# Decayed keys and queries of the RWKV chunks made inside the first attention, in other storage

## The reference, cut to what matters

```
decay = exp(-exp(w_log));  a = sigmoid(aaa_bias + xa @ w_aaa_up)
kk = k * k_k, each head divided by its length
k = k * (1.0 + (a - 1.0) * k_a)
per token:  sa = state @ (-kk)
            state = state * decay + sa * (kk * a) + v * k
            y = state @ r
```

## Time and profile before

| | us |
|---|---|
| median of 3 runs (lowest to highest) | 1201.37 (1200.52 to 1203.36) |
| the profiled execution, its own time | 1199.54 |
| its span, first to last instruction | 1197.7 |
| PE busy | 1124.4 |
| DVE busy | 797.2 |
| ACT busy | 589.7 |
| POOL busy | 122.8 |

### The profile page before, as it was taken

The page is one execution under the profiler, slowest core; times in us unless marked ns, Lnnn a source line. Parts: engine busy times, 40 slices in busy tenths (PEclk is TensorE's granted clock), DMA queues, the critical chain, the costliest instruction groups (busy, mean ns, idle before and its releaser), DMA issues.

```text
span 1197.7 us, 18403 instructions
## 1 busy us (share of the span) xinstructions
PE 1124.4 (94%) x7620; PEld 918.8 (77%) x7620; DVE 797.2 (67%) x1319; ACT 589.7 (49%) x911; POOL 122.8 (10%) x122
## 2 busy tenths in 40 slices
PE   7898799999999999999998999999998799999997
PEld 5666678787888888887877778878777677888785
DVE  5647774658666776557567895778768868455644
ACT  6465333254556564465755644453563266345441
POOL 0404161400000000000000000003405400000000
PEclk9999799999999999999999999999998899999998
DMA  8522112224555455455322644555531244555551
GB/s 304 190 93 101 36 54 72 72 88 155 171 187 187 165 185 181 166 182 185 127 86 102 246 165 155 189 191 183 182 116 38 72 159 154 189 184 186 193 186 52
DMA packets 49668, 177.50 MB, mean 148 GB/s; under 512 B 5648, under 2 KB 6288, under 8 KB 49328
## 3 DMA queue, kind: packets, MB, share of 16 engines
q1 hardware_dynamic: 49584, 176.32, 42.1%
HBM read 175.25 MB, written 1.05 MB: 147 GB/s over the span
## 4 chain that ended last, share of the span: by engine, by line
PE 75%; DVE 13%; ACT 7%; issue 2%; POOL 1%; DMA 1%; SPq 0%; DVEq 0%; ACTq 0%
PE wps L2632 21%; PE wps L2634 20%; PE wps L2633 20%; PE tps L2621 4%; DVE wlo L1777 3%; ACT whi L1392 2%; DVE bt L2386 1%; PE tps L2862 1%; PE tps L2867 1%; DVE bt L2397 1%; POOL arena L2451 1%; PE tps L2678 1%; PE tps L3042 1%; DMA x<-in_x 1%; PE tps L2839 1%
## 5 line engine op out<-in xcount | busy, mean ns | idle before, releaser
L1777 DVE TENSOR_TENSOR wlo<-raw,whi 128x1024 fp32r<-128x1024 f32 (+1 forms) x322 | 390.5, 1237 | 170.3 <-ACT whi L1392 169.1
L2632 PE MATMUL wps<-whi,a_hi 128*128 128x512 f32 (+1 forms) x1008 | 404.4, 401 | 20.4 <-DVE a_lo L1799 8.4
L2634 PE MATMUL wps<-wlo,a_hi 128*128 128x512 f32 (+1 forms) x1008 | 395.1, 392 | 0.0
L2633 PE MATMUL wps<-whi,a_lo 128*128 128x512 f32 (+1 forms) x1008 | 394.4, 391 | 0.0
L1392 ACT ACTIVATE whi<-raw 128x1024 fp32r<-128x1024 f32 (+1 forms) x322 | 325.4, 1050 | 53.6 <-PE wps L2634 50.6
L2632 PEld LDWEIGHTS wps<-whi,a_hi 128*128 128x128 f32 x1008 | 191.5, 190 | 66.3 <-DVE wlo L1777 13.9
L2634 PEld LDWEIGHTS wps<-wlo,a_hi 128*128 128x128 f32 x1008 | 190.9, 189 | 40.5
L2633 PEld LDWEIGHTS wps<-whi,a_lo 128*128 128x128 f32 x1008 | 191.7, 190 | 36.7
L2632 PE MATMUL wps<-whi,f_hi 128*128 128x512 f32 x264 | 104.8, 397 | 0.0
L2634 PE MATMUL wps<-wlo,f_hi 128*128 128x512 f32 x264 | 104.3, 395 | 0.0
L2633 PE MATMUL wps<-whi,f_lo 128*128 128x512 f32 x264 | 104.3, 395 | 0.0
(11 more groups left out here) (404 smaller groups left out, 1261.9 us busy)
## 6 DMA issues: line engine op xcount, KB each, us to landing
raw<-in_w_dn SPq DMA_DIRECT2D x22, 512.0 KB, 3.2
raw<-in_w_0dn SPq DMA_DIRECT2D x22, 512.0 KB, 3.2
raw<-in_w_1dn SPq DMA_DIRECT2D x22, 512.0 KB, 3.2
raw<-in_w_ua SPq DMA_DIRECT2D x20, 512.0 KB, 3.2
raw<-in_w_ub SPq DMA_DIRECT2D x20, 512.0 KB, 3.6
raw<-in_w_0ug SPq DMA_DIRECT2D x20, 512.0 KB, 3.2
raw<-in_w_0uu SPq DMA_DIRECT2D x20, 512.0 KB, 3.3
raw<-in_w_1ug SPq DMA_DIRECT2D x20, 512.0 KB, 3.2
```

The costliest lines, as they stand in the source:

```text
L1777: V.tensor_tensor(t.wlo[n % NR][:, 0:w], t.raw[n % NR][:, 0:w], t.whi[n % NH][:, 0:w].bitcast(F32), ALU.subtract).then_inc(m.done(s.dve_lo ...
L2632: T.matmul(o, xh, wh, start=first, stop=False)
L2633: T.matmul(o, xl, wh, start=False, stop=False)
L2634: mm = T.matmul(o, xh, wl, start=False, stop=last)
```

## The change

`decayed` becomes a generator among the RWKV preparations, put behind the shifted tiles of `wr`, with two tiles at each of its two steps. It no longer waits for `heads_out` 1. `AR` moves to `h`, the tile of the residual stage, `btl` and `ktl` stay at 28 and 32 KB of the arena, where the attention had rotary scratch, and the probabilities that lay there get other storage. The `fill` behind the four `decayed` goes away with them.

```diff
+    def decayed_prep():
+        for t in range(4):
+            emit("decayed", t, z_parts["wr"])
+            if t % 2:
+                yield
+
...
-                                       ("wr", "zr", 512, 0, None), ("wv", "zv", 512, 8, bonus_prep)):
+                                       ("wr", "zr", 512, 0, decayed_prep), ("wv", "zv", 512, 8, bonus_prep)):
...
-    for t in range(4):
-        emit("decayed", t, z_parts["wr"])
-    fill(1)
...
-        t.mprob = [view(24, 384), view(25.5, 384), view(34, 384), sb("mprob3", [P, 384], F32, s1)[:, :]]
-        t.mprobT = [view(27, 384), view(28.5, 384)]
+        t.mprob = [view(24, 384), view(25.5, 384)] + [sb(f"mprob{i}", [P, 384], F32, s1)[:, :] for i in (2, 3)]
+        t.mprobT = [view(42, 384), sb("mprobT1", [P, 384], F32, s1)[:, :]]
...
-        t.AR = view(20, 2048).rearrange("p (t c a s) -> p t c a s", t=4, c=2, a=2)
+        t.AR = t.h[:, :, :].rearrange("p j c -> p (j c)").rearrange("p (t c a s) -> p t c a s", t=4, c=2, a=2)
...
     def decayed(i, z):
         dve.wait_ge(*m.at("ka"))
         dve.wait_ge(*m.at("Wn"))
-        dve.wait_ge(*m.at("heads_out", "m", 1))
...
     def decayed(i, z):
         pool.wait_ge(*m.at("k2"))
         pool.wait_ge(*m.at("Wn"))
-        pool.wait_ge(*m.at("heads_out", "m", 1))
```

## The result

The changed kernel takes 1205.43 us (median of 11 runs, 1203.39 to 1206.67) against 1201.09 for the kernel before (11 runs, 1198.11 to 1204.33). The medians differ by 4.3 us. The ratio is 1.0031, interval 1.0022 to 1.0040; 0.31% of the time is 3.7 us. The median lies outside the range given. The profiled execution has a span of 1202.0 us.

A forecast was written before the change was run, and what follows sets the result against it. PE was taken to bound the kernel, with DVE setting the pace at the attention's end. Terms -2.7 - 1.4 + 2.8 + 0.8 = -0.5 us gave 1200.9 us; forecast's own range 1199.2 to 1203.2, with outer cases 1198.0 to 1204.2.

The forecast's parts named there:

- DVE's queue: End of the first attention: DVE's twelve operations take 4.0 us there, making wv's tiles late by 3.9 us.
- The moved slab: Behind rwkv_out of chunk 1: a third slab with nothing to hide under, cost 2.8 us, bounds 0 and 3.0.
- So this wait hides behind DVE: In the attention: values 4 waits for heads_out 0's bank until 130.7 us, at no cost because DVE is later.
- parts two and three: DVE's operations lengthen the attention by 4.0 us; behind it key_tokens start 2.7 us earlier and the clock gains 1.4.
- An equal rise puts it near 140: End of the attention: PE's clock rises near 140 us, so key_tokens and pair scores gain 1.4 us.
- part four: Later slabs shift: one more uncovered behind rwkv_out of chunk 1 costs 2.8 us, the moved empty steps 0.8 together.
- +0.75 with the way there and back: Behind right_side of chunk 1, now without a slab: solve waits for ACT's copy of RU, cost 0.75 us.
- The signs: Wrong if key_tokens start outside 142 to 146, clock is low at g0's first slab, or y_mean outside 257 to 262.
- (2): Clock stays low through key_tokens, pair scores and following slabs: +3.7 us (1205.1), with two slabs +6.5; chance 0.10.
- (3): Attention ends as late as key_tokens start now: +2.2 us, up to +5.9 (1203.6 to 1207.3); chance 0.08.
- (1): Slab finds a hole, or DVE's twelve are hidden: -3.3 or -3.5 us (1198.1 or 1197.9); chance 0.18.
- the term of 0: POOL's early ktl beside DVE's split: split and copy grow 1.6 us, taken as free before DVE's 2.15 us idle.

The follow-up runs named there:

- e9: Changed kernel with all four decayed in the formerly empty step behind probs_T 4, no shifted steps, and the slab behind the attention kept; 1200.39 us, 0.9994 to before.
- e5: As e1, plus the two new preparation steps, which emit nothing; 1201.19 us, 0.9998 to before.
- e1: Changed kernel's new storage and no wait for heads_out, but decayed at its old place with its fill; 1199.0 us, 0.9975 to before.
- e12: Changed kernel plus 32 matmuls with unused results in PE's waits of the attention; 1203.93 us, 1.0013 to before.
- e3: Changed kernel with one slab more behind the takes at right_side of chunk 1, taken from the three at the end; 1201.06 us, 0.9996 to before.
- e4: The changed kernel run again, code unchanged; 1205.5 us, 1.0028 to before.
- e6: Against before: new storage, btl, ktl and AR's key half two steps after key_mix, query half behind heads_out 1; 1200.84 us, 0.9987.
- e10: Third profile of the kernel before, code unchanged; y_mean 143.3 us after the scores of heads 6 and 7, against 140.2 in the first profile.
- e13: e8 plus 7, 6 and 6 matmuls with unused results in PE's waits of the attention; 1196.30 us, 0.9958 to before.
- e8: e1 with DVE making btl ahead of AR, and each tile's pair scores waiting only for that tile's AR; 1196.47 us, 0.9963 to before.

## Why the prediction was wrong

**What held.** DVE's queue: the twelve operations stand 0.335 us apart between 130.02 and 135.01, with heads_out 0 in their middle; wv's tiles are 3.75 us late against the scores (forecast 3.9). key_tokens have no wait. Pair scores and key_tokens run at full clock, which gains 1.6 us (forecast 1.4). The moved slab turns up uncovered at the end, three in a row before y_mean. The wait ahead of solve is 0.90 us (forecast 0.75).

**"So this wait hides behind DVE" held too.** values 4 waited 2.65 us for the bank, but v_tokens began 16.07 us behind the scores, exactly as in e9, which has the operations and not the shift. What the prediction left out is that the shift costs something by itself: in e5, without the operations, v_tokens come 1.0 us later and the last values 2.3 later than in e1. How much of that is the bank (0.63 us of waiting), how much the order, and how much the clock, no run separates.

**First failed step, in parts two and three: "An equal rise puts it near 140".** The lower clock lasted from 128.2 to 145.3 us, 17.1 us where before has 10.3. Counted from the scores the rise came at 22.6 us; the forecast's 140 is 19.8. values 5 stood ahead of bonus_sum at half clock, and bonus_sum took 3.73 us where the sum had 2.2. The attention ended 5.0 us late in place of 4.0. I had carried the time of a rise over from one order of work to another. e12 shows that the low clock is the cause: with PE kept busy bonus_sum takes 1.97 and v_tokens 1.06, and the attention ends 2.4 us behind before. Why the rise comes so late stays open. It isn't the idle time alone: between the scores and v_tokens PE's waits add up to 8.5 us in e9 and to 7.8 in the change, and in e9 the clock rises at 19.0. Nor is it fixed by the code: in e3, with the same attention, it rose at 20.4, and the last values came 3.9 us late, which is the forecast.

**Second and larger, part four: "+0.75 with the way there and back".** The wait was priced, what it does to the clock was not. Solve ran at the lower clock, in part or wholly, and so did the slab behind it, in each of the three profiles of after and in e12; e3 puts a slab there and has neither. From right_side of chunk 1 to y_mean both kernels do the same work, four slabs among it: 19.9 us before (240.46 to 260.33), 22.3 after (242.35 to 264.69), so 2.5 us are lost there.

**The sum.** By the landmarks of the first profiles the pair scores are over 3.4 us earlier (forecast 4.1), the slab costs 2.8 as forecast, and the rest 2.5 (forecast 0.8): +1.9 for -0.5. The medians say +4.3 and the ratio +3.7. The first profile of before is one of the shortest. The four profiles of before have y_mean at 260.3, 259.9, 264.7 and 263.1 us from the start of the span (262.0 on average), the three of after at 264.7, 265.0 and 264.3 (264.7). That is 2.6, of which 1.5 lie ahead of the scores, where PE has the same work in both, and 1.1 behind them. What remains, 1.1 to 1.7 us, lies behind y_mean, where the code is the same. The 99 runs of before in the four later comparisons have 50 us of low clock each on average, the 23 of after in the first two 60 (2 x span x (1 - mean clock)); the first profile of before has 43 by this count and its second 41. Among the 99 runs of before themselves, those with 10 us more of low clock take about 2.5 us longer (a fitted line). So the rest goes together with low clock in other places; with so few profiles its cause stays open.

**The signs.** The prediction called itself wrong for key_tokens outside 142 to 146 us and y_mean outside 257 to 262 (its first transposes). As they stand, 147.3 and 263.8, both fall outside. With the 2.5 us by which the scores are late taken off, key_tokens (144.9) lie inside and y_mean (261.3) just inside. The clock is full at the first slab of g0.

**Rivals.** (2) named the clock but put it behind key_tokens, where it was full; low clock lasted longer ahead of them and came again 100 us later. That its price, 3.7 us, is the measured one is luck. (3), that key_tokens don't come earlier, is refuted: they came 1.8 us earlier. (1) is refuted: the operations were not hidden (e9, v_tokens 3.75 us late), and the slab cost its 2.8.

**The overlap with POOL.** The split is DVE L1780, beside POOL's four. In the first profile of after it began just ahead of POOL's third (120.05 and 120.10) and took 1.22 us; that POOL operation took 1.76 where the median is 0.74. In e4, the same code, it began behind POOL's third (120.41 and 120.25) and took 1.66, and in e1 1.71. In e6 two of DVE's operations took 0.94 to 0.96 in place of 0.41. That the later one waits is what the Trainium skill says ("SBUF — State Buffer", "Who interferes with whom"), and the trace agrees. DVE idled 1.70 us behind the split even in e4, and nobody waited for POOL, so the term of 0 held.

**The clock.** The Trainium skill's "TensorE: Matmul & The Clock Gate", Part 1, was weighed for a gain only. That idling drops the clock bears on the hole ahead of solve as well, and there it speaks against the change. The traces agree as far as they go: low clock followed the 0.90 us of waiting in four of four profiles. But e10 has it at right_side with no such wait, so the wait is not its only cause.

## What to carry to other kernels

Price a new wait of PE together with the clock behind it: here a hole of 0.9 us behind a chain of small matmuls cost about 2.5, and a slab put into it took that back. A step moved into a stretch where DVE sets the pace comes out at its full length; move what frees a buffer or an engine (here the wait and the storage) apart from the order, and measure the two alone, since here the first gained 0.25% and the second lost more than 0.5%. When a change is worth less than the spread of one kernel's executions, take its places from several profiles and count them from the last instruction ahead of the change that both kernels share, and compare the low clock of all runs, not of one profile each.

## What was not expected of the hardware

Executions of one kernel, instruction for instruction the same, differ in where the lower clock falls: none near 53 us in two profiles of before, 6.8 us in one and 3.4 us in one; 3.4 or 6.8 us near 112 us; and on right_side of chunk 1 in one of four. The medians of before (1200.5 to 1201.7) lie 1.0 to 2.2 us above its first two profiled executions (1199.5), and that is of this size. Putting 19 matmuls into PE's waits (e13) brought the low clock between 119 and 270 us to zero in its profile (10.2 in e8), and the runs' average over the whole span from 48 to 38 us, for a gain too small to be told from none.
